# Seven of the eight pointwise units of a convolution block move high and low rows together

## The reference

```python
def conformer_conv(h, pw1, pw1_b, dw, dw_b, ln_w, ln_b, pw2, pw2_b):
    u = jax.nn.glu(h @ pw1 + pw1_b, axis=-1)
    u = lax.conv_general_dilated(u, dw[:, None, :].astype(u.dtype), (1,), [(CONV_WIDTH - 1, 0)],
                                 dimension_numbers=('NWC', 'WIO', 'NWC'),
                                 feature_group_count=D_MODEL) + dw_b
    u32 = u.astype(jnp.float32)
    mean = jnp.mean(u32, axis=-1, keepdims=True)
    var = jnp.mean(jnp.square(u32 - mean), axis=-1, keepdims=True)
    u = ((u32 - mean) * lax.rsqrt(var + LN_EPS) * ln_w.astype(jnp.float32) + ln_b.astype(jnp.float32)).astype(h.dtype)
    return jax.nn.silu(u) @ pw2 + pw2_b
...
            x = x + conformer_conv(h, *mix_params[layer])
        x = x + sq_relu_mlp(rmsnorm(x, g_ffn), up, down)
```

## Time and profile before

| what | value |
|---|---|
| time, median of 3 runs (lowest to highest) | 962.73 us (959.42 to 964.07) |
| profiled execution: its own time, and its span | 959.6 us, 957.8 us |
| TensorE busy | 921.5 us (96%) |
| VectorE busy | 642.8 us (67%) |
| ScalarE busy | 458.4 us (48%) |
| GpSimd busy | 73.5 us (8%) |
| mean granted TensorE clock | 0.994 of full |

### The profile page before, as it was taken

The page is one execution under the profiler, slowest core; times in us unless marked ns, Lnnn a source line. Parts: engine busy times, 40 slices in busy tenths (PEclk is TensorE's granted clock), DMA queues, the critical chain, the costliest instruction groups (busy, mean ns, idle before and its releaser), DMA issues.

```text
span 957.8 us, 15427 instructions
## 1 busy us (share of the span) xinstructions
PE 921.5 (96%) x6358; PEld 792.3 (83%) x6358; DVE 642.8 (67%) x858; ACT 458.4 (48%) x658; POOL 73.5 (8%) x149
## 2 busy tenths in 40 slices
PE   6999999999999999999899999999999799999997
PEld 5888788899899988888688888888985588888886
DVE  5579788677768966746476656667655866666655
ACT  6445465434567444421364454545542755444453
POOL 6000000000110030000000000000553000000000
PEclk9999999999999999999999999999999899999999
DMA  9855444555665541000156665565893256566631
GB/s 324 250 183 176 132 165 144 176 176 188 219 199 176 179 130 45 1 1 3 45 176 219 193 204 176 176 192 160 251 229 90 68 174 220 176 190 207 196 111 44
DMA packets 106085, 152.42 MB, mean 159 GB/s; under 512 B 4114, under 2 KB 82464, under 8 KB 106016
## 3 DMA queue, kind: packets, MB, share of 16 engines
q1 hardware_dynamic: 101424, 141.19, 45.3%
q0 software_dynamic: 4272, 9.85, 3.8%
q10 hardware_dynamic: 320, 0.40, 0.1%
HBM read 145.58 MB, written 1.06 MB: 153 GB/s over the span
## 4 chain that ended last, share of the span: by engine, by line
PE 89%; DVE 6%; ACT 3%; issue 1%; DMA 0%; POOL 0%; SPq 0%; DVEq 0%; ACTq 0%; POOLq 0%
PE banks L1981 21%; PE banks L1934 14%; PE banks L1935 13%; PE banks L1936 13%; PE banks L1982 11%; PE banks L2324 4%; PE banks L2552 2%; DVE wl L1104 1%; PE banks L2412 1%; PE banks L2093 1%; PE banks L2117 1%; PE banks L2043 1%; ACT wh L656 1%; DVE x L1172 1%; PE banks L2423 1%
## 5 line engine op out<-in xcount | busy, mean ns | idle before, releaser
L1104 DVE TENSOR_TENSOR wl<-raw,wh 128x2048 fp32r<-128x2048 f32 x130 | 297.6, 2291 | 113.6 <-ACT wh L656 113.0
L656 ACT ACTIVATE wh<-raw 128x2048 fp32r<-128x2048 f32 x132 | 252.2, 1913 | 135.8 <-PE banks L1936 93.1
L1981 PE MATMUL banks<-x,wh 128*128 128x512 f32 x896 | 314.8, 394 | 0.0
L1982 PE MATMUL banks<-x,wl 128*128 128x256 f32 x896 | 250.5, 280 | 0.0
L1981 PEld LDWEIGHTS banks<-x,wh 128*128 128x128 f32 x896 | 168.2, 188 | 39.6 <-issue 3.0
L1982 PEld LDWEIGHTS banks<-x,wl 128*128 128x128 f32 x896 | 168.4, 188 | 1.1
L1934 PE MATMUL banks<-wh,yh 128*128 128x512 f32 x290 | 114.0, 393 | 3.0 <-DVE yl L1660 3.0
L1936 PE MATMUL banks<-wh,yl 128*128 128x512 f32 x290 | 112.5, 388 | 0.0
L1935 PE MATMUL banks<-wl,yh 128*128 128x512 f32 x290 | 112.5, 388 | 0.0
L1934 PE MATMUL banks<-x,wh 128*128 128x256 f32 x320 | 92.1, 288 | 1.8 <-DVE x L1172 1.7
L1936 PE MATMUL banks<-x,wl 128*128 128x256 f32 x320 | 90.1, 282 | 0.0
(11 more groups left out here) (375 smaller groups left out, 1248.5 us busy)
## 6 DMA issues: line engine op xcount, KB each, us to landing
raw<-in_l_ffn_up SPq DMA_DIRECT2D x32, 1024.0 KB, 5.5
raw<-in_l_ffn_down SPq DMA_DIRECT2D x32, 1024.0 KB, 4.9
raw<-in_w_in SPq DMA_DIRECT2D x29, 1024.0 KB, 5.1
raw<-in_l_w_in SPq DMA_DIRECT2D x13, 1024.0 KB, 5.1
raw<-in_l_pw SPq DMA_DIRECT2D x12, 1024.0 KB, 5.4
arena<-arena POOLq DMA_DIRECT2D x64, 71.0 KB, 4.2
raw<-in_w_out SPq DMA_DIRECT2D x4, 1024.0 KB, 5.1
raw<-in_l_w_out SPq DMA_DIRECT2D x4, 1024.0 KB, 5.0
```

Source lines behind the costliest of these rows:

```text
L656: nc.scalar.activation(wh[:, u % WBUFS, :], raw[:, u % RAWS, :], ACT.Copy).then_inc(E("hi_split"), 1)
L1104: nc.vector.tensor_tensor(wl[:, u % WBUFS, :], raw[:, u % RAWS, :], wh[:, u % WBUFS, :].bitcast(F32), ALU.subtract).then_inc(E("lo_split"), 1)
L1981: mm(outs[t], h[:, k, c], x2[:, k, :, :].rearrange("p w t -> p (w t)"), start=k == 0, stop=False)
L1982: ins = mm(outs[t][:, 0:T], l[:, k, c], xh[:, k, :], start=False, stop=k == KC - 1)
```

## The change

pa0 stays a narrow unit in bank 0. The other seven units (pb0, pa1 to pb3) become wide: pa{i} in banks 0 and 1, pb{i} in banks 2 and 3. VectorE adds the two halves of each bank and writes the sums to `ytmp` or `thb`; then it waits for its own sums and multiplies them in place by the tokens' reciprocal norms. ScalarE, which used to wait for the bank to be emptied, waits for this product (`rows_scaled_out`). The taps keep banks 4 to 7.

```diff
     for i in range(4):
-        s.unit("T", "l1_pw1_2", 0, 256 * i, s.use(f"pa{i}"))
-        s.unit("T", "l1_pw1_2", 0, DM + 256 * i, s.use(f"pb{i}"))
+        if i == 0:
+            s.unit("T", "l1_pw1_2", 0, 0, s.use("pa0", 0))
+        else:
+            wide(f"pa{i}", "l1_pw1_2", 256 * i, 0)
+        wide(f"pb{i}", "l1_pw1_2", DM + 256 * i, 2)
         s.use(f"taps{i}", 4 + i)
...
                     if tag == "pb":
                         next_unit()
-                    wait_empty(act, f"{tag}{i}")
+                    if (tag, i) == ("pa", 0):
+                        wait_empty(act, "pa0")
+                    else:
+                        act.wait_ge(E("rows_scaled_out"), 2 * i + (tag == "pb"))
...
+            def summed_and_scaled(dst, name):
+                wide_sum(dst, name)
+                wait_empty(dve, f"{name}_0"), wait_empty(dve, f"{name}_1")
+                nc.vector.tensor_tensor(dst, dst, rows2, ALU.mult).then_inc(E("rows_scaled_out"), 1)
+
...
                     wait_empty(dve, "rb4")
+                    scaled_out(chunks(ytmp[:, 0, :]), "pa0")
                 else:
                     dve.wait_ge(E("glu"), i)
-                scaled_out(chunks(ytmp[:, 0, :]), f"pa{i}")
+                    summed_and_scaled(chunks(ytmp[:, 0, :]), f"pa{i}")
                 next_unit()
-                scaled_out(chunks(thb[:, 0, 0:512]), f"pb{i}")
+                summed_and_scaled(chunks(thb[:, 0, 0:512]), f"pb{i}")
                 glu(i)
...
                 else:
-                    t_unit(f"pa{i}")
-                t_unit(f"pb{i}")
+                    wide_unit(f"pa{i}")
+                wide_unit(f"pb{i}")
                 if i == 2:
                     conv_taps(0)
```

## The result

| | median us | lowest to highest | runs |
|---|---|---|---|
| before | 962.65 | 959.42 to 964.07 | 8 |
| changed | 967.13 | 963.42 to 969.76 | 8 |

The ratio is 1.0047, 95% interval [1.0027, 1.0067]: 4.5 us slower, with an interval of 2.6 to 6.4 us. The forecast was 967.1 us. The profiled execution of the changed kernel spans 963.0 us, against 957.8.

A forecast was written before the change was run, and what follows sets the result against it. It took VectorE's serial loop with ScalarE to bound this stage, though TensorE is 96% busy. taps3 3.4 us later, less 0.5 us of old idle, plus 1.5 us of clock: +4.4 us on 962.73, 967.1 us, range 962.5 to 969.9.

The forecast's parts named there:

- wide unit: TensorE's pointwise products: a wide unit takes 5.56 us against 5.80 for a narrow one; seven save 1.7 us.
- one scaling longer by: VectorE's scaling: a second sum (0.60 us) and the wait for it before the product (0.73 us) add 1.33 us.
- wait before pb2: TensorE waits 0.9 us because pb2 writes banks 2 and 3, which VectorE is still summing for pb1.
- old idle that goes: Behind taps3, TensorE's 0.49 us idle for ln_square_sum disappears, as its VectorE work runs during the new idle.
- The serial loop: VectorE to ScalarE to VectorE, glu to glu: a chain not waiting for TensorE, growing from 12.34 to 15.0 us.
- VectorE's idle behind taps0: VectorE's waits for taps0 (2.48 us) and pa3 (1.45 us) vanish, paying for 4.1 of 9.3 us added.
- Part 4: Late glu 3 delays GpSimd's 16 row copies; TensorE idles 4.2 us before taps3, net +2.9 us.
- Part 5: TensorE's clock falls in the idle before taps3; some 3 us run at half rate: +1.5 us, bounds 0 to 3.5.
- rival (b): Same stall before taps3, but TensorE's clock stays up: +2.9 us, 965.6 us; chance 32%.
- rival (c): Clock low for all of taps3's first half, or parts of both halves: +6.4 us, 969.1 us; chance 13%.
- Rival (a): TensorE bounds throughout, no new idle: 961.9 us; needs under about 0.74 us added per scaling; chance 8%.
- Rival (d): Wide units as long as narrow ones on TensorE; time equal to the forecast's, so no chance of its own.

The follow-up runs named there:

- a single move on ScalarE: Changed kernel with ScalarE's high split of the second unit moved ahead of pa's bias steps: 960.93 us, ratio 0.9983; repeated, 959.75 us, ratio 0.9969.
- the delay alone: Kernel before, narrow products, with two extra VectorE sums (result overwritten) ahead of each of seven scalings: 966.84 us, ratio 1.0046.
- the filled idle: Changed kernel with 16 unread products of 512 columns put on TensorE in its idle ahead of taps3: 965.22 us, ratio 1.003.
- The run with 0.72 us per scaling: Kernel before, narrow products, with one extra VectorE sum (result overwritten) ahead of each of seven scalings: 963.37 us, ratio 1.0008.

## Why the prediction was right

| step | forecast | measured |
|---|---|---|
| wide unit | 5.56 us, 1.7 us saved in seven | 5.60 and 5.64 us, 1.40 us (wide units without sums) |
| one scaling longer by | 1.33 us | 1.39 us (1.28 row, then 1.39 to the product) |
| loop | 15.0 us | 15.14 us |
| glu(3) later by | 5.2 us | 5.63 us |
| wait before pb2 | 0.9 us | 0.77 us |
| idle before taps3 | 4.2 us | 4.04 us |
| taps3 later by | 3.4 us | 3.82 us |
| old idle that goes | 0.49 us | 0.65 us, from 1.19 to 0.54 between the two sum products |
| clock | 1.5 us | 1.6 us |
| stage | +4.4 us | +4.64 us |

**The serial loop** was the step on which all hung, and it held: both idle brackets kept their length, and a single move on ScalarE took out 2.9 of the 15.1 us. **VectorE's idle behind taps0** paid for 4.1 us of the added 9.7 (7 x 1.39, of which 5.63 reached glu(3)); the runs with three wide units show it from both sides. **Part 4** held in each link: the delay alone gave the loss (4.2 us), and splitting the copies over two queues took 3.5 of the 4.64 us away with glu(3) as late as ever. **Part 5** was the least certain step, since 0 to 3.5 us were open and rival (b) had 32%. The clock did fall, and the filled idle puts its price at 1.58 us. It fell 3.8 us into the idle and not 2.3, close to the landing of the copies, which is the condition that the forecast gave for rival (c). The price stayed that of the forecast because the clock came back 3.1 us after the products began: that term of the forecast (3.0 us) held, and the dearer reading, twice the time for all 64 products, did not come. That it fell in the profiled executions of both kernels with an idle of 2.7 or 4.0 us, and did not at 2.09 us, is what the traces hold; how often it falls over many executions no run here tells.

**What was off:** small terms. The price of the dependent product was short by 0.06 us, seven times; that is the 0.4 us by which glu(3) and taps3 were later than forecast, and it moved the time. The wide unit was taken too short (5.56 us against 5.60 and 5.64), because the units next to the taps have a longer distance at either end; it would have mattered only in rival (a). TensorE was also not as early at taps3 as I had it: lnc's product came 0.36 us earlier than before, not 0.8. The wait before pb2 reads 0.77 us, but lnc's product stands at S + 56.81, 1.04 us behind the run without sums (S + 55.77), so the wait costs more than its bracket. None of these last three moved the time, because the copies decide it. The stage came out 0.24 us above the forecast. That the median fell on 967.1 us to the decimal is luck: its interval is 1.9 us to either side.

**Rival (a)** gave the point from which the lateness counts: 0.74 us per scaling. For narrow units, whose cover is the full 1.9 us, the same sum gives (4.1 + 1.9) / 7 = 0.86 us. The run with 0.72 us per scaling lies a little below it and shows no loss; that with 1.32 us shows a loss of 4.2 us. Where between them the loss begins no run shows, and the slow landing above says that the 0.86 us are not sharp. **Rival (d)** was that the wide units save nothing; they save 1.40 us.

## What to carry to other kernels

An engine that is busy for 67% may have no time to give: follow its timeline round one loop and see whether its idle brackets are released by engines that in turn wait for it. If they are, as here, added operations lengthen the loop by their full time (2 x 1.39 us on VectorE, 2.80 us on the loop), and a remedy is to reorder the chain, as one moved instruction did. Then look for who stands behind the last result of the loop (here 8.5 us of copy issues) and how much cover they have: up to it lateness is free, beyond it one pays for the wait and, where dense products followed, for TensorE's clock too (1.6 us before taps3, nothing before pw2).

## What was unexpected of the hardware

- **SyncE's issues of these row copies** were slower than GpSimd's: 8 in 5.99 us (0.59 us at least, one of 1.35) against 0.54 us each from GpSimd, while SyncE's issues of the 1 MB weight loads show 0.37 us. In that run copies of both queues landed later, too: 3.0 to 3.6 us for GpSimd's last three against 1.9 to 2.0.
- **The clock's fall has no fixed distance from the start of an idle.** It came 2.3 us into one of 6.21 us (before), 2.5 us into one of 2.68 us (narrow products with two more sums) and 3.8 us into one of 4.04 (changed); one of 2.09 us (two queues) passed without it.
- **A wait on TensorE costs more than its bracket:** 0.77 us of idle before pb2 put lnc's product 1.04 us behind the run without sums, which has no such wait, and 1.02 us behind the run with the sums and the high split first, which has none either.
- **The scatter between executions lies ahead of this stage.** S moves by 6.4 us over the thirteen profiles, while the 210 us from E to the end agree within 0.2 us.
